# The input products of the feed-forward and recurrent stages from the fourth tile on: normalised rows and one 512-column product in place of raw rows scaled afterwards

## The reference, cut to what matters

```
for layer in range(2):
    sh1, sc1, g1, sh2, sc2, g2 = split(silu(c) @ ada_w[layer] + ada_b[layer], 6)
    hh = rms_norm(x, norm1_g[layer]) * (1.0 + sc1) + sh1
    mix = nsa_mixer(hh, ...) if layer == 0 else rglru_mixer(hh, ...)     # rglru: hh @ rg_w_in
    x = x + g1 * mix
    hh = rms_norm(x, norm2_g[layer]) * (1.0 + sc2) + sh2
    x = x + g2 * swiglu(hh, ffn_w_in[layer], ffn_w_out[layer])           # (silu(hh@Wg) * (hh@Wu)) @ Wo
```

## Time and profile before

| | us |
|---|---|
| median of 3 runs (lowest, highest) | 1641.22 (1635.0, 1641.47) |
| span of the profiled execution (its own total is not listed) | 1637.1 |
| TensorE busy | 1423.5 (87%) |
| VectorE busy | 797.9 (49%) |
| ScalarE busy | 544.4 (33%) |
| GpSimd busy | 27.3 (2%) |

### The profile page before, as it was taken

How to read it: one execution, slowest core, us unless ns; L and a number is a source line. 1 busy time by engine, 2 the same in 40 slices (tenths; PEclk the granted TensorE clock), 3 DMA queues, 4 the chain that set the end, 5 groups by cost and what they waited for, 6 DMA issues and landing times.

```text
span 1637.1 us, 26662 instructions
## 1 busy us (share of the span) xinstructions
PE 1423.5 (87%) x11182; PEld 1107.4 (68%) x11182; DVE 797.9 (49%) x1326; ACT 544.4 (33%) x803; POOL 27.3 (2%) x35
## 2 busy tenths in 40 slices
PE   5999998999978765565565799999999999999999
PEld 3889886677953221121121487569999999999999
DVE  4443336666731100000000578657776477877753
ACT  3432124555310100000000452655443366754431
POOL 1100000000000000000000000000000001200000
PEclk8999999999979987787778799999999999999999
DMA  9855447565679999999999965844555545445520
GB/s 397 342 231 206 155 172 310 213 232 230 241 296 378 429 427 427 428 428 428 426 428 428 376 248 224 350 171 165 181 182 186 187 166 181 162 173 182 184 99 27
DMA packets 49279, 437.71 MB, mean 267 GB/s; under 512 B 5264, under 2 KB 7696, under 8 KB 8336
## 3 DMA queue, kind: packets, MB, share of 16 engines
q1 hardware_dynamic: 48160, 430.99, 66.6%
q10 hardware_dynamic: 1008, 5.09, 0.8%
HBM read 435.00 MB, written 1.05 MB: 266 GB/s over the span
## 4 chain that ended last, share of the span: by engine, by line
PE 67%; DMA 20%; DVE 6%; ACT 3%; issue 3%; PEld 0%; SPq 0%; POOL 0%; PEldq 0%; DVEq 0%; ACTq 0%; POOLq 0%
PE bank L833 60%; DMA ring<-in_w 18%; PE bank L1252 3%; PE bank L837 2%; PE bank L1280 2%; DMA ring_end<-in_w 1%; ACT ring_r L1625 1%; DVE arena L2293 0%; DVE ring_end_r L2001 0%; DVE arena L2134 0%; ACT arena L1737 0%; DVE ring_r L2001 0%; DVE stat L2162 0%; ACT ring L1675 0%; PEld bank L833 0%
## 5 line engine op out<-in xcount | busy, mean ns | idle before, releaser
L833 PE MATMUL bank<-arena_r,ring_r 128*128 128x256 f32 (+1 forms) x5032 | 701.2, 284 | 13.5 <-DVE H_r L1970 5.0
L833 PEld LDWEIGHTS bank<-arena_r,ring_r 128*128 128x128 f32 x5032 | 654.3, 191 | 28.4 <-issue 10.6
L2001 DVE TENSOR_TENSOR ring_r<-ring,ring_r 128x2048 fp32r<-128x2048 f32 x107 | 244.1, 2284 | 161.3 <-ACT ring_r L1625 161.0
L1252 PE MATMUL bank<-ring,arena 128*32 128x512 f32 x960 | 156.5, 786 | 106.6 <-DMA ring<-in_w 104.9
L1625 ACT ACTIVATE ring_r<-ring 128x2048 fp32r<-128x2048 f32 x107 | 203.1, 1900 | 109.0 <-PE bank L833 104.7
L833 PE MATMUL bank<-H_r,ring_r 128*128 128x256 f32 x800 | 183.5, 290 | 3.3 <-DVE H_r L1962 3.3
L1252 PEld LDWEIGHTS bank<-ring,arena 128*32 128x32 f32 x960 | 30.3, 128 | 218.1 <-DMA ring<-in_w 157.5
L833 PEld LDWEIGHTS bank<-H_r,ring_r 128*128 128x128 f32 x800 | 136.5, 196 | 6.9 <-issue 6.4
L2293 DVE TENSOR_TENSOR arena<-arena,bank 64x512 f32<-64x512 f32 x16 | 11.1, 691 | 242.3 <-ACT arena L1737 242.3
L1737 ACT ACTIVATE arena<-bank 64x512 f32<-64x512 f32 x16 | 9.4, 590 | 328.4 <-PE bank L1252 328.4
L833 PE MATMUL bank<-arena_r,ring_end_r 128*128 128x256 f32 (+1 forms) x384 | 109.5, 285 | 0.0
(11 more groups left out here) (316 smaller groups left out, 1399.7 us busy)
## 6 DMA issues: line engine op xcount, KB each, us to landing
ring<-in_w SPq DMA_DIRECT2D x91, 2048.0 KB, 25.5
ring<-in_w SPq DMA_DIRECT2D x169, 1024.0 KB, 4.9
ring_end<-in_w SPq DMA_DIRECT2D x47, 1024.0 KB, 4.9
arena<-in_w SPq DMA_DIRECT2D x5, 1024.0 KB, 10.0
ring<-in_bias ACTq DMA_DIRECT2D x1, 2048.0 KB, 12.3
H<-in_w SPq DMA_DIRECT2D x2, 1024.0 KB, 12.2
ring_end<-in_w SPq DMA_DIRECT2D x1, 2048.0 KB, 18.7
consts<-in_consts ACTq DMA_DIRECT2D x1, 1199.0 KB, 9.4
```

The source lines that it names most:

```text
L833: i = nc.tensor.matmul(o, lhsT, rhs, start=start, stop=stop, skip_group_check=grouped)
L1252: last = matmul(bank[0][32 * j:32 * j + 32, :], x_now(e, k), columns(slot_of(c), j, 512), start=k == 0, stop=k == KT - 1)
L2001: v.tensor_tensor(r(lo), lo, r(hi), ALU.subtract).then_inc(lo_ready, 1)
```

## The change

Three `apply` steps (norms 4, 5 and 6) are added to the list, each between tile 0 and tile 1 of its stage. Tiles 0, 1 and 2 stay as they are. From tile 3 on (`NORMED` = 3) TensorE uses `normed_tiles`: for each k and half one product of the high weights with all 512 columns of `H`, so that columns 0 to 255 of the bank get high x low and columns 256 to 511 high x high, and one of the low weights with the 256 columns of `H_HI`, which is added to columns 0 to 255. ScalarE copies columns 256 to 511 of both banks to SBUF, VectorE adds columns 0 to 255 to them. Norm and shift are already in, so VectorE's copies of the shift column and its multiplies by the norm go, the bias of the activation is 0, and the Identity in the recurrent stage goes.

```diff
@@ plan_steps
-    s += [("ffn_in", 0, i) for i in range(FFN_T)] + [("ffn_end", 0)] + ...
+    s += [("ffn_in", 0, 0), ("apply", 4)] + [("ffn_in", 0, i) for i in range(1, FFN_T)] + [("ffn_end", 0)] + ...
-    s += [("rnn_in", i) for i in range(RNN_T)] + [("rnn_end",)]
+    s += [("rnn_in", 0), ("apply", 5)] + [("rnn_in", i) for i in range(1, RNN_T)] + [("rnn_end",)]
...
@@ build
-        H_COUNT = {0: 16, 3: 24}
+        H_COUNT = {0: 16, 3: 24, 4: 32, 5: 40, 6: 48}
@@ TensorE
             def h_is(ni, k=KT - 1):
-                if ni == 3:
-                    pe.wait_ge(h_split, 16 + k + 1)
+                if ni >= 3:
+                    pe.wait_ge(h_split, H_COUNT[ni] - KT + k + 1)
...
+            def normed_tiles(x):
+                hi, lo = split_chunk(x, 8)
+                begin(x)
+                b = [bank[JOBS[x].bank], bank[JOBS[x].bank + 1]]
+                for k in range(KT):
+                    if x[-1] == NORMED:
+                        h_is(NORM_BEFORE[x[:-1]], k)
+                    for j in range(2):
+                        n = slice(j * P, (j + 1) * P)
+                        mm(b[j][:, :], r(hi[:, k, n]), r(H[:, k, :]), k == 0, False, grouped=True)
+                        mm(b[j][:, 0:T], r(lo[:, k, n]), r(H_HI[:, k, :]), False, k == KT - 1,
+                           job_done if j == 1 and k == KT - 1 else None, True)
+                owed[0] += 1
@@ ScalarE
+            def copy_halves(x, gate, up):
+                job(x)
+                f(gate, bank[JOBS[x].bank][:, T:2 * T], ACT.Copy)
+                f(up, bank[JOBS[x].bank + 1][:, T:2 * T], ACT.Copy).then_inc(half_copied, 1)
             def step_ffn_in(l, i):
+                if i >= NORMED:
+                    act.wait_ge(ffn_ready, FFN_T * l + i - 1)
+                    copy_halves(("ffn_in", l, i), ffn_g[:, i % 2, :], ffn_p[:, i % 2, :])
                 act.wait_ge(in_scaled, in_no(("ffn_in", l, i)))
-                f(ffn_g[:, i % 2, :], ffn_g[:, i % 2, :], ACT.Silu, bias=in_shift(i)[:, 0:1]).then_inc(ffn_silu, 1)
+                shift = in_shift(i)[:, 0:1] if i < NORMED else 0.0
+                f(ffn_g[:, i % 2, :], ffn_g[:, i % 2, :], ACT.Silu, bias=shift).then_inc(ffn_silu, 1)
             def step_rnn_in(i):
+                if i >= NORMED:
+                    copy_halves(("rnn_in", i), gelu_g[:, i, :], u_in[:, i, 3:T + 3])
                 act.wait_ge(emptied["dve"], JOBS[("rnn_in", i)].emptied)
+                if i < NORMED:
                     v = u_in[:, i, 3:T + 3]
                     f(v, v, ACT.Identity, bias=in_shift(i)[:, 1:2]).then_inc(act_step, 1)
                     own[0] += 1
...
@@ VectorE, scale_tile
+                if x[-1] >= NORMED:
+                    dve.wait_ge(half_copied, copied_no(x))
+                    v.tensor_tensor(gate, b[0][:, 0:T], gate, ALU.add).then_inc(in_scaled, 1)
+                    takes(v.tensor_tensor(up, b[1][:, 0:T], up, ALU.add), x)
+                    return
@@ VectorE, multiply
+                if i < NORMED:
                     link(v.scalar_tensor_tensor(p, p, in_shift(i)[:, 1:2], ffn_g[:, i % 2, :], ALU.add, ALU.mult))
+                else:
+                    link(v.tensor_tensor(p, p, ffn_g[:, i % 2, :], ALU.mult))
```

More of the change, by code:

```diff
@@ L41 @@
 CHUNK = 2048
+NORMED = 3
 SLOTS, CYCLE, HOMES = 14, 12, 8
@@ L172, in plan_steps @@
     s += lifted(4, ("ffn_in", 0))
-    s += [("ffn_in", 0, i) for i in range(FFN_T)] + [("ffn_end", 0)] + [("ffn_out", 0, j) for j in range(FFN_T // 2)]
+    s += [("ffn_in", 0, 0), ("apply", 4)] + [("ffn_in", 0, i) for i in range(1, FFN_T)] + [("ffn_end", 0)] + [("ffn_out", 0, j) for j in range(FFN_T // 2)]
     for p in range(4):
@@ L184, in plan_steps @@
     s += lifted(6, ("ffn_in", 1))
-    s += [("ffn_in", 1, i) for i in range(FFN_T)] + [("ffn_end", 1)] + [("ffn_out", 1, j) for j in range(FFN_T // 2)]
+    s += [("ffn_in", 1, 0), ("apply", 6)] + [("ffn_in", 1, i) for i in range(1, FFN_T)] + [("ffn_end", 1)] + [("ffn_out", 1, j) for j in range(FFN_T // 2)]
     s += [("ffn_add", 1, p) for p in range(4)]
@@ L631, in build @@
         xa_half, xa_ready, in_scaled = sem("xa_half"), sem("xa_ready"), sem("in_scaled")
+        half_copied = sem("half_copied")
         ffn_ready, u_ready = sem("ffn_ready"), sem("u_ready")
@@ L689, in in_no, with copied_no @@
             return {("ffn_in", 0): 0, ("rnn_in",): FFN_T, ("ffn_in", 1): FFN_T + RNN_T}[x[:-1]] + x[-1] + 1
+        def copied_no(x):
+            return in_no(x) - NORMED * {("ffn_in", 0): 1, ("rnn_in",): 2, ("ffn_in", 1): 3}[x[:-1]]
         def squares_of(ni, p):
@@ L915, in xa_tiles, with in_tiles @@
                 owed[0] += 1
+            def normed_tiles(x):
[11 more added lines that the diff above has]
+                owed[0] += 1
+            def in_tiles(x):
+                if x[-1] >= NORMED:
+                    normed_tiles(x)
+                elif x[-1]:
+                    xa_tiles(x)
             def sum_part(ni, ks):
@@ L1462, in step_ffn_in @@
             def step_ffn_in(l, i):
-                if i:
-                    xa_tiles(("ffn_in", l, i))
+                in_tiles(("ffn_in", l, i))
             def step_first_in(*name):
@@ L1490, in step_rnn_in @@
             def step_rnn_in(i):
-                if i:
-                    xa_tiles(("rnn_in", i))
+                in_tiles(("rnn_in", i))
             seen = [-1]
@@ L1827, in step_nsa_t @@
                     takes(o, ("nsa_t", i, half))
+            def copy_halves(x, gate, up):
+                job(x)
+                f(gate, bank[JOBS[x].bank][:, T:2 * T], ACT.Copy)
+                f(up, bank[JOBS[x].bank + 1][:, T:2 * T], ACT.Copy).then_inc(half_copied, 1)
             def step_ffn_in(l, i):
+                if i >= NORMED:
+                    act.wait_ge(ffn_ready, FFN_T * l + i - 1)
+                    copy_halves(("ffn_in", l, i), ffn_g[:, i % 2, :], ffn_p[:, i % 2, :])
                 act.wait_ge(in_scaled, in_no(("ffn_in", l, i)))
-                f(ffn_g[:, i % 2, :], ffn_g[:, i % 2, :], ACT.Silu, bias=in_shift(i)[:, 0:1]).then_inc(ffn_silu, 1)
+                shift = in_shift(i)[:, 0:1] if i < NORMED else 0.0
+                f(ffn_g[:, i % 2, :], ffn_g[:, i % 2, :], ACT.Silu, bias=shift).then_inc(ffn_silu, 1)
             own = [0]
             def step_rnn_in(i):
+                if i >= NORMED:
+                    copy_halves(("rnn_in", i), gelu_g[:, i, :], u_in[:, i, 3:T + 3])
                 act.wait_ge(emptied["dve"], JOBS[("rnn_in", i)].emptied)
[L1837 to L1840, removed]
+                if i < NORMED:
+                    v = u_in[:, i, 3:T + 3]
+                    f(v, v, ACT.Identity, bias=in_shift(i)[:, 1:2]).then_inc(act_step, 1)
+                    own[0] += 1
+                shift = in_shift(i)[:, 0:1] if i < NORMED else 0.0
+                f(gelu_g[:, i, :], gelu_g[:, i, :], ACT.Gelu_apprx_tanh, bias=shift)
                 act.wait_ge(act_step, own[0])
@@ L2466, in multiply @@
                 p = ffn_p[:, i % 2, :]
-                link(v.scalar_tensor_tensor(p, p, in_shift(i)[:, 1:2], ffn_g[:, i % 2, :], ALU.add, ALU.mult))
+                if i < NORMED:
+                    link(v.scalar_tensor_tensor(p, p, in_shift(i)[:, 1:2], ffn_g[:, i % 2, :], ALU.add, ALU.mult))
+                else:
+                    link(v.tensor_tensor(p, p, ffn_g[:, i % 2, :], ALU.mult))
                 link(v.tensor_copy(r(ffn_h[:, i, :]), p))
```

## The result

The changed kernel is slower by 0.27% (ratio to before 1.0027, 95% interval 1.0017 to 1.0038; 1641.96 us median of 7 runs beside 1637.86 us of 7 runs of before on the same chip). That is 4.4 us; I had forecast 4.3 us the other way. The total of 1637 us that I forecast stood on a before of 1641.2 us, the median of three runs, where seven give 1637.9: that base, 3.4 us too high, hides part of the miss, which is 5 us in the total and 8.4 us in the difference of the medians.

What follows compares the result with a forecast made beforehand. TensorE was taken to bound the edited stages; -17.0 us from products, +9.5 from waits and +3.2 from clock falls make -4.3, so 1641.2 becomes 1637 us, range 1625 to 1651.

Steps and rivals of the forecast that it cites:

- TensorE bounds, and the tile is 48 x 119.8 ns: Edited stages before the change: TensorE sets the pace, a feed-forward input tile of 48 products taking 5.75 us.
- The pace does not follow the columns; streaming hides under a cost of 110 to 120 ns: TensorE's products: something once per product, with its weight load, sets 110 to 120 ns; twice the columns cost 9% more.
- The long product at 216 ns: New 512-column product, priced from the gates' block: pair 336 ns, tile 5.38 us, 46 tiles save 17.0 us.
- rival D: Unhidden fixed cost, 13 ns added to every product: long 227 ns, tile 5.54, 9.5 us gained, total 1644 us; chance 14%.
- The short product at 120: New 256-column product between two long ones keeps 120 ns, as the next product's weights load under it; lower bound 108 ns.
- Case B: Rival: the short product hides too, at 108 ns; tile 5.18 us, 25 us gained, total 1629 us; chance 24%.
- ScalarE's copies are covered; the loop is 5.0 us: VectorE-ScalarE loop per tile: copies (0.8 us) fall within VectorE's 2.2 us lower half; 5.0 us stays under TensorE's 5.38.
- The fourth tile waits 2.9, 3.7 and 2.9 us: Fourth tile of each edited stage: TensorE waits behind apply, together 9.5 us, bounds 6 and 13.
- The clock falls after two of three: After the three TensorE waits: two falls to 1.2 GHz at 1.6 us each, 3.2 us, bounds 0 and 4.8.
- The sum: Whole change: -17.0 + 9.5 + 3.2 = -4.3 us, from a median of 1641.2 to 1637 us.

Runs made afterwards that it cites:

- e8: Kernel with apply spread in pieces behind tiles 0 to 6, with each normalised tile's 16 long products before its 16 short ones: ratio 1.0 to before, stretch 510.9 us.
- e7: On e2, the long product done as two of 256 columns with the same weights loaded twice: stretch 510.9 us, -1.3 against before.
- e3: On e2, a stationary operand of 64 instead of 128 columns in the new products: 230 and 118 ns, 5.59 us a tile, stretch 504.8 us.
- e6: On e2, the long product cut from 512 to 384 columns: 176 ns, tiles at 4.70 us, after 12 tiles 4.92.
- e1: Changed kernel with apply done but no tile using H, all keeping the 258-column products: ratio 1.0084 to before, stretch 525.6 us, +13.4.
- e5: Changed kernel with 20 idle products of 256 columns before the fourth tile's waits in each stage: ratio 1.0023 to before, stretch 514.6 us.
- e11: e5 run once more unchanged, on another chip: stretch 513.7 us; 5.65 us a tile in stage 4, 5.55 in stages 5 and 6.
- e9: e8 with the first normalised tile of each stage keeping the alternating long, short order: ratio 0.9971 to before, 1631.57 us beside 1636.34, stretch 506.7 us.
- e2: Changed kernel without the three apply steps, the new products reading raw input rows: ratio 0.9968 to before, stretch 506.3 us, -5.9.

## Why the prediction was wrong, by its own steps

- **TensorE bounds, and the tile is 48 x 119.8 ns.** Right.
- **The pace does not follow the columns; streaming hides under a cost of 110 to 120 ns.** Wrong, and the ground of the next step: in e8, from 256 to 512 columns, a column costs 0.418 ns, which is streaming at 2.4 GHz, and 13 to 15 ns come on top of it. That 128 columns take 110 ns does not follow from this sum, and no run looked into it.
- **The long product at 216 ns: wrong, and this is the step that failed.** It takes 227 in a row of equals, 230 to 236 between short ones. I took the price from the gates' records, plain fp32 products of 256 columns, and read their 216 ns as 512 cycles of streaming with 2.9 ns on top. The fp32r rows had a cost of 13.3 ns of their own at 256 columns, and it stays at 512. The saving was 9.3 us, not 17.0: rival D's size and cause, to which I gave 14%. I had set D aside because 258 columns cost no more than 256. With more digits they cost 0.6 ns more (119.7 and 119.2, e7), near D's 0.8; my two figures, 119.8 and 120, were too coarse to be used so.
- **The short product at 120.** 115 to 118 behind a long one, 120 in a row. Nearly right: the 3 ns less, over 16 products in 46 tiles, are 2 us in the change's favour. Case B did not occur. The Trainium skill ("TensorE: Matmul & The Clock Gate", "Back-to-back issue gap") has 2.5 ns beyond streaming; for these fp32r products the runs show 13 to 15 and the measurement decides. The same section calls that formula the gap of an isolated product, not of a stream as I had put it, and says that in a real stream weight load and product set the spacing together; e3 found no trace of the load's width in the spacing, within 2 ns.
- **ScalarE's copies are covered; the loop is 5.0 us.** Right: 4.92 in e6, no wait of TensorE in the steady part.
- **The fourth tile waits 2.9, 3.7 and 2.9 us.** Nearly: 2.56, 3.44, 2.56, in the place and by the queue order named; 8.6 in place of 9.5. Two thirds of the difference in stage 4 are that tiles 1 and 2 take 11.73 us in both kernels, not the 11.5 that I had counted.
- **The clock falls after two of three.** It fell after all three, in both kernels with the waits, at the price foreseen (1.5 to 1.7 us for 1.6): 4.8 in place of 3.2.
- **The sum.** -9.3 + 8.6 + 4.8 = +4.1, measured +4.2 in the stretch and +4.4 in the runs. The bound, the waits and the falls were right in kind, and the errors of the last two (-0.9 and +1.6) partly cancel. The gain, mis-sized by 7.7 us because a product's own cost was taken to hide, turned the sign.

## What to carry to other kernels

Take the price of a product you have not seen from products of the same number format, at another size, and split it into a slope and a constant: fusing two products saved the constant here, not the part of the stream that seemed hidden. A step put in front of a queue costs whoever waits behind it what the lead does not cover: `apply` held VectorE for 6.4 us in stage 4 (from 1128.53) and TensorE waited 2.56. Each wait of TensorE of some 2.6 us cost its length and nearly two thirds again by the clock; the same work in pieces caused no wait and no fall, though fewer tiles then had the new products (34 of 55 in place of 46). And check how much of a small gain is left when the step that makes it possible is paid: here 9.3 us against 13.4.

## What the runs showed of the hardware that I had not expected

- In the edited stages distances of 2.68 to 3.56 us between the starts of two products were followed by a fall to 1.2 GHz each time (six of six, in the changed kernel and in e1), and the clock stayed low for 3.4 us; distances of 1.5 and 2.2 us (e8), and 1.2 us (stage 5 of e5 and of e11), were not (five of five). Nothing measured here lies between 2.2 and 2.68.
- One long wait is not the only thing that lets the clock fall. In the sparse attention, ahead of the edited stages, the clock of the changed kernel fell at 1085.5 us, though for 20 us no two products had been more than 0.97 us apart; TensorE had several short waits there. Twelve of the fourteen traces have this fall, before and e9 do not. Windows of the changed kernel, the first just before the fall:

```profile
1082.00:1085.50 3.50, 2.20 (x19) 1.23 (x19) 3.21 (x12) 3.50 (x14) 0.00 (x0) 0.99 0.07 30
1085.50:1089.00 3.50, 3.50 (x23) 2.62 (x20) 0.85 (x2) 0.20 (x2) 0.00 (x0) 0.52 0.00 0
```

- A long and a short fp32r product in turn have more than one pace: 5.55 or 5.65 us a tile, fixed for a whole stage, and different from one execution to the next of the same kernel (e5 and e11, on two chips). With raw rows it was 5.62 (e2) and 5.59 (e3). Sixteen of a kind in a row had one pace, 5.57, in all nine stages in which they ran. Ordering equal products together made the tile's time the same in each of these stages; why the alternating order has two is open.
